# A routed-expert stage with 96 token columns per expert in place of 88

## The chip, the cores and the metric

The kernel runs on one core of one Trainium2 chip. The metric is device time in microseconds of one execution, the median of the runs. The profile is of one more execution of the same program, taken by the hardware profiler. Everything is float32.

## The reference, cut to what matters

A two-layer network is applied to 128 prompt tokens and 128 latent tokens. The second layer ends in a mixture of experts, and the change lies there:

```
logits = (xt @ w_router)                       # 8 experts
top_v, top_i = lax.top_k(logits, TOP_K)        # TOP_K = 2
top_w = jax.nn.softmax(top_v, axis=-1)
gate = sum(one_hot(top_i, N_EXPERTS) * top_w[..., None], axis=1)
for e in range(N_EXPERTS):
    out = out + gate[:, e:e+1] * swiglu(xt, wg[e], wu[e], wd[e])
# swiglu(x, wg, wu, wd) = (silu(x @ wg) * (x @ wu)) @ wd
```

The model width is 1024 and the hidden width of an expert is 2816. Each token goes to two of the eight experts, so 256 tokens make 512 pairs of token and expert, 64 per expert on average.

## The kernel before, in words

The two token groups run side by side (`NST = 2`, 256 tokens). Weights come through a ring of 11 tiles in SBUF (`ring`, `RING = 11`) of 1 MB each. The sync engine (SP) issues each tile's transfer when the slot's last reader has counted up `tile_used` and `tile_used0` (lines 433 to 441), and TensorE waits for the landing in `arrived` (line 607).

The expert stage works in units. A unit is one expert with room for `CAP` tokens: `SEL` is a 0/1 matrix that picks the tokens, `gather` (line 1362) multiplies by it to put up to `CAP` token columns into `XG`, and all that follows for the unit is `CAP` columns wide. Were an expert to have more than `CAP` tokens, the table built on VectorE (`OVER`, line 2629) would add further units for the same expert, which fetch the expert's weights once more. The loops run over units 0 to 6 and then from 7 to the number in the table, at least 8 and at most 13.

In a unit the hidden width is cut into steps of 1024, 1024, 512 and 256. Each step has a gate product and an up product (`across`, line 1394) and a down product (line 1415). All of them hold a 128x64 piece of a weight tile as the stationary operand and stream the token columns. They come in twos, one for each half of the 128 output rows (`HALVES`), so that the two halves of the array work at the same time. A float32 product is two records in the trace, so one pass of `for hp in HALVES` is two pairs of records. A tile is 64 records, a unit is 33 tiles or 2112 records, and eight units are 16896 records or 8448 pairs.

Between the products stand `turn_y` (line 1370, transposes of the unit's output before), `scatter` (line 1376, the output spread back over the tokens, twice two products of 512 columns), two transposes of `SEL` (line 1437), and the next unit's `gather`. ScalarE takes the gate products out of PSUM through SiLU (line 1878) and copies `YT`, `YG`, `SELT` and `XG`. VectorE multiplies by the up products (line 2664), adds the scattered output to `O` (line 2671), and makes the next `SEL` (line 2682). The order on each engine is the order of the code. The first seven units are unrolled on TensorE, so its program there is one long straight stream.

The block offsets in PSUM are multiples of `CAP`: four blocks side by side in a bank of 512 columns.

Of the kernel before, what the change touches and what calls it, by code (L numbers as in the profile page):

```python
# [38 lines left out]
NE = 8  # L39


CAP = 88
UNITS = NE + 5
STEPS = (1024, 1024, 512, TW)
UT = 33
# [129 lines left out]
def program(nc, t, out):  # L175
    ctx = ExitStack()
    with ctx:
        def sb(name, shape, dt=F32):
            return ctx.enter_context(nc.sbuf_tensor(name, shape, dt))
# [184 lines left out]
        TBL = sb("tbl", [P, 16], I32)  # L364
        SILU = W[5][:, 0:KC * CAP].rearrange("p (b n) -> p b n", b=2)
        HIDU = W[0][:, 0:2 * KC * CAP].rearrange("p (b c n) -> p b c n", b=2, c=KC)
        XG = W[1][:, 0:KC * CAP].rearrange("p (c n) -> p c n", c=KC)
        YG = W[1][:, 1024:2048]
        YT = W[4][:, 0:KC * CAP].rearrange("p (c n) -> p c n", c=KC)
        HTM = W[2][:, :].rearrange("p (s n) -> p s n", s=NST)  # L370
# [8 lines left out]
        IOTA = ROUTE[:, 384:512]  # L379
        SEL = ROUTE[:, 512:512 + NST * CAP].rearrange("p (s n) -> p s n", s=NST)  # L380
        SELT = ROUTE[0:CAP, 768:1024].rearrange("p (s n) -> p s n", s=NST)

# [2342 lines left out]
```

How the kernel before makes its waits and increments, by code:

```python
        @block.sync  # L427
# [3 lines left out]
            def tile(parts, i=None, per=0, dues=0):  # L431
                n = walk.n
                s, _ = walk.next(len(parts))
                if i is not None:
                    sp.wait_ge(sem("tile_used"), i * per + (n - RING + 1))
                    sp.wait_ge(sem("tile_used0"), i * per + (n - RING + 1))
                elif n >= RING:
                    sp.wait_ge(sem("tile_used"), tile_freed(tile_before(n)))
                for dst, src in parts:
                    sp.dma_start(dst(ring[:, s, :]), src).then_inc(sem(f"slot{s}"), 16)
# [49 lines left out]
            tile([whole(0, 1024, t["rw_w2"][0].rearrange("d k n -> (d k) n"))])  # L491
            tile([cols(t["rw_w_r"][0], TW)])
            tile([whole(0, 1024, t["rw_a2"][0], 64)])
            for n in range(2, 4):
                tile([cols(t["rw_w_r"][0], n * TW)])
            for n in range(4):
                tile([cols(t["rw_w_v"][0], n * TW)])
            tile([whole(0, 1024, t["rw_g2"][0])])
            for n in range(4):
                tile([cols(t["rw_w_o"][0], n * TW)])
            sp.wait_ge(sem("y"), 2 * KC)
            sp.wait_ge(sem("trk_done"), KC)
            ada_group(11)
            tile([(lambda s: s[:, 0:KC * NE].rearrange("p (k n) -> p k n", k=KC), kp(t["moe_router"][0]))])
# [31 lines left out]
                expert_tiles(u, u)  # L536
            walk.n = n0
            sp.wait_ge(sem("table"), 1)
            with sp.Fori(NE - 1, sp.value_load(TBL[0:1, UNITS:UNITS + 1], min_val=NE, max_val=UNITS)) as u:
```

## Time and profile before

| | us |
|---|---|
| median of 3 runs | 1753.9 |
| lowest and highest | 1748.24 and 1754.79 |
| the profiled execution's own time | 1753.9 |
| its span, first to last instruction | 1752.1 |
| TensorE busy | 1604.5 (92%) |
| VectorE, ScalarE, GpSimd busy | 530.2, 297.4, 16.4 |
| products of lines 1394 and 1415, busy | 448.9 and 224.6 |
| granted TensorE clock, mean | 0.970 |

The expert stage is the last 790 us of the span. The page's line of slices shows it as the stretch where the DMA digit is 9 from slice 22 on, where TensorE is also at 9, and where VectorE and ScalarE are at 0 and 1. Two numbers that look alike are not: the mean time of a product (240 ns) is how long one is under way, and the products overlap, so their pace is read from how many start in a stretch.

### The profile page before, as it was taken

The page shows a single profiled execution, that of the slowest core. Times are in us where ns is not written, and L with a number is a line of the kernel's source. Part 1 is how long each engine was busy: PE and PEld are TensorE (multiplying, and loading weights), DVE is VectorE, ACT ScalarE, POOL GpSimd, SP SyncE. Part 2 cuts the span into 40 slices and gives each one's busy share as a digit, 9 for nine tenths or more (in the row PEclk, how much of TensorE's full clock was granted, in tenths as well). Part 3 has the DMA queues.
Part 4 walks back from the last instruction along what each step waited for, and adds up shares of the span by engine and source line. Part 5 has one row for each costly group of instructions (what it writes and reads, how often), then busy time and mean ns, then how long its engine had stood idle before and what let it go on. Part 6 is the DMA issues. An engine that isn't in the chain of part 4 may idle for free.

```text
span 1752.1 us, 59234 instructions
## 1 busy us (share of the span) xinstructions
PE 1604.5 (92%) x27345; PEld 1420.5 (81%) x27345; DVE 530.2 (30%) x1253; ACT 297.4 (17%) x684; POOL 16.4 (1%) x32
## 2 busy tenths in 40 slices
PE   3999898999979999999687999999999999999996
PEld 1888477999447888898577989898989899898885
DVE  0363425667453436656524100000010101000001
ACT  1111413101023413343204001010100000010001
POOL 1000000000000000000000000000000000000000
PEclk9999998999999999999886999999999999999998
DMA  9832697545584420000433999999999999999990
GB/s 333 257 97 76 205 305 240 187 151 192 170 255 117 132 73 5 5 7 7 140 108 142 340 382 347 365 347 366 359 363 362 367 366 374 366 360 371 333 338 25
DMA packets 212032, 408.94 MB, mean 233 GB/s; under 512 B 13090, under 2 KB 135252, under 8 KB 211796
## 3 DMA queue, kind: packets, MB, share of 16 engines
q1 hardware_dynamic: 207344, 398.91, 64.1%
q8 instruction: 215, 3.52, 0.8%
q0 software_dynamic: 1184, 3.41, 0.7%
q10 hardware_dynamic: 3268, 2.93, 0.5%
q14 instruction: 21, 0.17, 0.0%
HBM read 403.30 MB, written 1.92 MB: 231 GB/s over the span
## 4 chain that ended last, share of the span: by engine, by line
PE 47%; PEld 40%; issue 5%; DVE 4%; ACT 2%; SPq 1%; DMA 1%; DVEq 0%; POOL 0%; PEldq 0%; ACTq 0%
PEld bank L1394 25%; PEld bank L1415 12%; PE bank L945 8%; PE bank L976 4%; PE bank L631 3%; PE bank L628 3%; PE bank L722 3%; PE bank L725 2%; PE bank L1155 2%; PE bank L1115 2%; PE bank L656 2%; PE bank L747 2%; PE bank L1151 2%; PE bank L1140 2%; PE bank L1091 2%
## 5 line engine op out<-in xcount | busy, mean ns | idle before, releaser
L1394 PEld LDWEIGHTS bank<-w,ring 128*64 128x64 f32 x11264 | 435.7, 137 | 43.0 <-issue 42.2
L1394 PE MATMUL bank<-w,ring 128*64 128x88 f32 x11264 | 448.9, 240 | 22.5 <-issue 21.5
L1415 PE MATMUL bank<-w,ring 128*64 128x88 f32 x5632 | 224.6, 240 | 11.7 <-issue 11.5
L1415 PEld LDWEIGHTS bank<-w,ring 128*64 128x64 f32 x5632 | 217.0, 137 | 17.9 <-issue 17.2
L2664 DVE TENSOR_TENSOR w<-w,bank 128x352 f32<-128x352 f32 (+1 forms) x48 | 22.1, 488 | 615.1 <-PE bank L1394 615.1
L1878 ACT ACTIVATE w<-bank 128x352 f32<-128x352 f32 (+1 forms) x48 | 19.3, 437 | 461.6 <-PE bank L1394 461.5
L628 PE MATMUL bank<-w,ring 128*128 128x256 f32 x256 | 57.6, 387 | 5.8 <-DVE w L2342 5.2
L656 PE MATMUL bank<-ring,ct 128*32 128x256 f32 x768 | 48.2, 405 | 15.7 <-DMA ring<-in_ada_w 14.0
L628 PEld LDWEIGHTS bank<-w,ring 128*128 128x128 f32 x256 | 49.4, 194 | 14.0 <-DVE w L2342 5.5
L631 PE MATMUL bank<-ring,w 128*128 128x256 f32 x256 | 58.1, 391 | 0.9 <-DVE w L1942 0.9
L631 PEld LDWEIGHTS bank<-ring,w 128*128 128x128 f32 x256 | 50.2, 197 | 8.5 <-DVE w L1942 1.3
L656 PEld LDWEIGHTS bank<-ring,ct 128*32 128x32 f32 x768 | 25.4, 116 | 35.3 <-issue 20.0
L1155 PE MATMUL bank<-ht 64*64 64x64 f32 x1280 | 49.7, 219 | 0.0
L2671 DVE SCALAR_TENSOR_TENSOR o<-bank,w,o 128x512 f32<-128x512 f32 x32 | 24.0, 751 | 84.3 <-PE bank L1376 82.2
L722 PE MATMUL bank<-ht,ring 128*128 128x256 f32 x192 | 45.3, 394 | 2.2 <-ACT ht L1532 2.2
L722 PEld LDWEIGHTS bank<-ht,ring 128*128 128x128 f32 x192 | 37.0, 196 | 8.3 <-ACT ht L1532 2.4
L1155 PEld LDWEIGHTS bank<-ht 64*64 64x64 f32 x1280 | 43.3, 135 | 0.5
L945 PE MATMUL bank<-ht,ring 128*128 128x128 f32 x352 | 43.0, 275 | 0.7 <-ACT gb L1539 0.7
L945 PE MATMUL bank<-w 128*128 128x128 f32 x352 | 42.9, 275 | 0.0
L945 PE MATMUL bank<-w,ring 128*128 128x128 f32 x352 | 42.9, 275 | 0.0
L725 PE MATMUL bank<-ring,ht 128*128 128x256 f32 (+1 forms) x192 | 41.9, 371 | 0.0
L945 PEld LDWEIGHTS bank<-ht,ring 128*128 128x128 f32 x352 | 41.1, 192 | 0.9 <-ACT gb L1539 0.9
(420 smaller groups left out, 1984.3 us busy)
## 6 DMA issues: line engine op xcount, KB each, us to landing
ring<-in_moe_w_gate SPq DMA_DIRECT2D x88, 1024.0 KB, 6.7
ring<-in_moe_w_up SPq DMA_DIRECT2D x88, 1024.0 KB, 7.1
ring<-in_moe_w_down SPq DMA_DIRECT2D x88, 1024.0 KB, 7.0
ring<-in_ada_w SPq DMA_DIRECT2D x48, 1024.0 KB, 6.2
ring<-in_ev_w_in SPq DMA_DIRECT2D x11, 1024.0 KB, 12.0
ring<-in_ffn_w_gate SPq DMA_DIRECT2D x11, 1024.0 KB, 7.8
ring<-in_ffn_w_up SPq DMA_DIRECT2D x11, 1024.0 KB, 5.3
ring<-in_ffn_w_down SPq DMA_DIRECT2D x11, 1024.0 KB, 6.5
```

What stands on the lines that cost most here:

```text
L628: ins = mm(b[:, a * TW:(a + 1) * TW], w[:, k, a * P:(a + 1) * P], src[:, k, :], start=k == 0, stop=k == KC - 1)
L631: ins = mm(b[:, a * TW:a * TW + n], src[:, k, a * P:(a + 1) * P], w[:, k, 0:n], start=k == 0, stop=k == KC - 1)
L656: ins = mm(sums_bank(n)[32 * j:32 * j + 32, 0:TW], CT[:, NST * k:NST * k + 32], w[:, k, :], start=k == 0, stop=k == KC - 1)
L722: ins = mm(b[:, a * TW:(a + 1) * TW], w[:, k, a * P:(a + 1) * P], HT[:, k, :], start=k == 0, stop=k == KC - 1)
L725: ins = mm(b[:, a * TW:a * TW + n], HT[:, k, a * P:(a + 1) * P], w[:, k, 0:n], start=k == 0, stop=k == KC - 1)
L747: ins = mm(bank[2 + 2 * (n % 2) + h][:, j * P:(j + 1) * P], KG[hp, seg], WQ[hp, seg] if lv else W[0][hp, qs], start=True, stop=True)
L945: ins = mm(region(j, r)[:, which * P:(which + 1) * P], lhs(which, k), rhs(k), start=first and which == 0 and k == 0, stop=k == 3, skip_gro ...
L976: ins = mm(bank[DOWN_BANK[p]][:, :], lhs, rhs, start=n == 0, stop=n == FT - 1)
L1091: ins = mm(bank[7 - n % 2][:, a * TW:(a + 1) * TW], XS["v"][:, k, a * P:(a + 1) * P], held["w"][:, k, :], start=k == 0, stop=k == KC - 1)
L1155: ins = mm(bank[2 + d][hp, (4 + j) * DH:(5 + j) * DH], IZ[hp, d, j, :], IP[i % 2][hp, d, j, :], start=True, stop=True)
L1394: ins = [mm(b[hp, (a % 4) * CAP:(a % 4 + 1) * CAP], w[:, k, a * P + hp.start:a * P + hp.stop], XG[:, kk, :], start=kk == 0 and a % 4 == 0, ...
L1415: ins = [mm(bank[4 + c // 4][hp, (c % 4) * CAP:(c % 4 + 1) * CAP], w[:, k, c * P + hp.start:c * P + hp.stop], HIDU[:, s % 2, 2 * part + k, :],
```

## The change

One constant is raised by eight. Every width that is written with `CAP` follows it: the streamed columns at lines 1362, 1394 and 1415, the width of the copies and multiplications at lines 1858, 1863, 1878, 1891, 2597, 2664 and 2682, the rows at 1370, 1376, 1437, 1883, 1886 and 1903, and the thresholds at lines 2629 and 2633. No instruction is added, removed or moved on any engine; all 803 rows of TensorE's order stand where they stood, with other sizes, and SP's order is the same word for word. Four blocks of 96 columns still fit in a bank of 512.

```
-CAP = 88
+CAP = 96
 UNITS = NE + 5
 STEPS = (1024, 1024, 512, TW)
```

## Rows read from the trace of the kernel before

**Rows 1.** The page: chain that ended last, by engine.
```profile
PE 47%; PEld 40%; issue 5%; DVE 4%; ACT 2%; SPq 1%; DMA 1%; DVEq 0%; POOL 0%; PEldq 0%; ACTq 0%
```

**Rows 2.** Windows: the expert stage, and 95 us of it; columns in the first line.
```profile
core 0: us, PE busy (x) PEld busy (x) DVE busy (x) ACT busy (x) POOL busy (x), PEclk, DMA share, GB/s
960.80:1731.10 770.30, 735.65 (x17296) 697.23 (x17296) 57.06 (x137) 62.02 (x118) 0.00 (x0) 1.00 0.94 347
1067.00:1162.00 95.00, 90.48 (x2130) 85.47 (x2128) 6.55 (x14) 8.07 (x15) 0.00 (x0) 1.00 0.97 359
```

**Rows 3.** The page: transfers by tensor, size, issue to landing.
```profile
ring<-in_moe_w_gate SPq DMA_DIRECT2D x88, 1024.0 KB, 6.7
```

**Rows 4.** Waits of SP's queue, 975 to 1731 us: total, times, longest.
```profile
SPq L437 <- PE bank L1394: 368.1, 168, 4.0
SPq L437 <- PE bank L1415: 193.5, 81, 7.0
```

**Rows 5.** TensorE's waits, 972.3 to 1731.1 us: total, times, longest.
```profile
PE bank L1394 <- issue: 21.5, 34, 1.8
PE bank L1415 <- issue: 11.5, 21, 1.2
PE bank L1362 <- issue: 0.9, 1, 0.9
```

**Rows 6.** Timeline, 1098 to 1135 us: start, us, what, idle before.
```profile
1103.58 1.12 PE L1415 MATMUL bank<-w,ring 128*64 128x88 f32 x23
...
1105.32 5.07 PE L1415 MATMUL bank<-w,ring 128*64 128x88 f32 x128 [0.62 <-issue]
1105.32 4.91 PEld L1415 LDWEIGHTS bank<-w,ring 128*64 128x64 f32 x128 [0.79 <-issue]
...
1117.02 5.07 PE L1394 MATMUL bank<-w,ring 128*64 128x88 f32 x127 [1.23 <-issue]
...
1128.25 5.07 PE L1415 MATMUL bank<-w,ring 128*64 128x88 f32 x128 [0.68 <-issue]
```

**Rows 7.** DMA queues, 975 to 1725 us: packets, MB, share.
```profile
q1 hardware_dynamic: 88451, 262.03, 93.9%
q8 instruction: 133, 2.18, 1.1%
```

**Rows 8.** DMA queues, 800 to 850 us.
```profile
q8 instruction: 11, 0.18, 1.6%
q10 hardware_dynamic: 540, 0.12, 1.3%
```

**Rows 9.** Timelines at three widths: 64, 88 and 512 columns.
```profile
807.32 0.63 PE L1151 MATMUL bank<-ht 64*64 64x64 f32 x16
807.79 0.63 PE L1155 MATMUL bank<-ht 64*64 64x64 f32 x16
...
985.73 9.93 PE L1394 MATMUL bank<-w,ring 128*64 128x88 f32 x256
995.59 1.98 PE L1376 MATMUL bank<-w 88*128 88x512 f32 x4
...
434.67 1.88 PE L976 MATMUL bank<-w 128*128 128x512 f32 x4
436.39 1.02 PE L976 MATMUL bank<-ring,w 128*128 128x512 f32 x2
```

**Rows 10.** Timelines: full weight loads with 128 and with 88 columns.
```profile
324.90 1.95 PE L945 MATMUL bank<-w 128*128 128x128 f32 x16
326.68 1.95 PE L945 MATMUL bank<-w,ring 128*128 128x128 f32 x16
...
1143.62 3.81 PE L1362 MATMUL bank<-w 128*128 128x88 f32 x32
```

**Rows 11.** Instructions by form, 972.3 to 1731.1 us: ScalarE, then VectorE.
```profile
L1878 ACT ACTIVATE w<-bank 128x352 f32<-128x352 f32 x40 | 16.8, 461 | 305.9 <-PE bank L1394 305.8
L1878 ACT ACTIVATE w<-bank 128x176 f32<-128x176 f32 x8 | 2.5, 317 | 155.7 <-PE bank L1394 155.7
...
L2664 DVE TENSOR_TENSOR w<-w,bank 128x352 f32<-128x352 f32 x40 | 19.4, 518 | 486.8 <-PE bank L1394 486.8
```

**Rows 12.** The last of the pauses, 1697 to 1706 us.
```profile
1702.48 3.02 PE L1394 MATMUL bank<-w,ring 128*64 128x88 f32 x73 [1.77 <-issue]
```

## The prediction

> **What bounds the kernel now.** I read the chain of waits first: 87% of it is TensorE and its weight loads [rows 1]. Then I cut out the stage that the change touches. The expert stage, from the first product of line 1394 to the last of line 1415, is 770.3 us of the span of 1752.1, TensorE is busy for 735.65 of them, and the transfers are at a share of 0.94 [rows 2]. Both look like a bound, and the whole case hangs on which it is.
>
> If transfers were the bound, wider products would hide behind them. They are not, and two views say so. SP spends 368.1 + 193.5 = 561.6 us of this stage waiting for TensorE to give back a slot, never more than 7.0 us at a time [rows 4]. So a tile is asked for when the one 11 places before it is done. It lands 6.7 us later in the median [rows 3]. A tile is 64 products, 2.43 us at the pace found below, so its turn comes more than 20 us after it was asked for, and it lies ready for some 15 to 20 us. The transfers run at TensorE's speed because TensorE gives out the slots. They are nearly full all the same, which matters below.
>
> How many units run? The gate weights are fetched 88 times, 11 tiles for each of 8 units [rows 3]. Eight is the least the table can give. No expert has more than 88 tokens, and the larger room saves nothing.
>
> **TensorE's pace by width.** Lines 1394 and 1415 put two products on the two halves of the array, and I count in pairs. At 88 columns 256 records start in (9.93 - 0.24) us, 128 pairs, 75.7 ns each (75.8 by the starts inside a run) [rows 9]. At 64 columns 16 records start every 0.47 us, 58.4 ns a pair. At 512 columns, one product at a time, four start in 1.72 us, 430 ns each [rows 9]. From 88 to 512 that is (430 - 75.8)/424 = 0.835 ns per column, two passes at 2.4 GHz, and 75.8 is 88 x 0.833 + 2.5. So what is streamed sets the pace at 88. The load of a 64-column weight is no bound there, since the same load fits in 58.4 ns at 64 columns. Hence 96 columns take 96 x 0.833 + 2.5 = 82.5 ns, 6.67 ns more per pair.
>
> Term 1: 8448 pairs x 6.67 ns = +56.3 us. Its bounds: the slope from 64 to 88 columns, 0.73 ns, gives 5.8 ns and +49; if the fixed part grew from 2.5 to the 5 ns seen at 64 columns, the pair takes 85.0 ns and the term is +78. I take +56.
>
> The Trainium skill has another figure for a stream of weight loads and products (TensorE: Matmul & The Clock Gate, "Back-to-back issue gap"): about 81 ns at 128 columns and 131 ns at 512, because the loads are pipelined with the products. By it a column costs 0.13 ns, 16 more streamed columns per pair (two passes) cost 2.1 ns, and the term would be 8448 x 2.1 = +18 us. The rows at 88 and 512 columns speak against it.
>
> **The pauses, which give some of it back.** TensorE is idle in the stage for 21.5 + 11.5 + 0.9 = 33.9 us in 56 pieces, all marked issue [rows 5]. It isn't the ring (tiles lie ready), and no engine releases it. The timeline shows what they are: 128 products with their 128 weight loads, a pause, 128 more, a pause [rows 6]. 256 instructions also are what one packet of the instruction queue brings: 133 packets move 2.18 MB, 16.4 KB each, 64 bytes an instruction [rows 7]. All but two of these pauses stand at the same place in a block of 256 instructions when the stream is counted from its start. The next block of TensorE's program is late. A product's record stays open for 0.24 us, so the true loss is some 0.17 us more per pause. Read off the starts it is 46 us, in 64 pauses of over 0.2 us from 979.9 to 1702.5 us, the longest 1.8 [rows 6, 12].
>
> A block of 128 products runs 64 x 75.8 = 4.85 us. Pauses of 0.6 us, the common ones, mean that a block took 5.4 to 5.5 us to come, and the long ones 6 to 6.6. In the scan at 800 to 850 us the same products' worth of instructions (128 at 29.2 ns, 3.7 us a block) came at 3.7 us without a pause, with the data queues at 1.3% [rows 8, 9]. So the fetch is slowed by the weight traffic that it shares the engines with.
>
> With 96 columns a block runs 64 x 82.5 = 5.28 us, 0.43 us longer. Each pause shrinks by that or goes. Done pause by pause over the 64, 51 stay, with 21 us in them. That is the upper value if the fetch is as slow as now. But TensorE then asks for a tile every 2.64 us of a run and not every 2.43, 397 GB/s and not 431, so the queue in front of the fetch is shorter. If that takes another 0.4 us from the fetch, 8 us remain; another 0.2, 13 us. The ends are 46 (nothing shrinks) and 0. I take 14.
>
> Term 2: 46 - 14 = 32 us given back.
>
> The Trainium skill (Runtime: NRT & Kernel Launch, "Instruction fetch mechanics") says that instructions come in blocks of 256 and that crossing a block boundary is mostly hidden. The block size is that of the rows; hidden it isn't here. If the pauses had another cause, as that would suggest, nothing would be given back, which is the second rival below.
>
> **The small edits.** The gather (32 products in 3.81 us) runs at 112 to 119 ns a product with 88 columns, the same as 111.7 ns for 128 columns with the same full load [rows 10], so its 8 more columns are free: bounds 0 and 9 gathers x 32 x 6.67 ns = 1.9 us, taken 0. The scatter streams 512 columns whatever `CAP` is. ScalarE's copies grow by (461 - 317)/176 = 0.8 ns a column, 26 ns for 32 more [rows 11]; VectorE's by about as much. Both engines are busy for 62 and 57 us of 770 and wait for TensorE [rows 2, 11]. The few copies that TensorE waits for, two at the start and four at the end of the stage, add 0.1 us. Selecting tokens before the stage has two instructions of 8 more columns, under 0.02 us. Loads are the same in number and size. Nothing before the stage changes.
>
> **The sum.** +56.3 - 32 + 0.2 (with the first 4 us of the stage at half clock) = +24.5 us. The profiled execution took 1753.9 us, as did the median, so 1778.5 us; the span would be 1776.6.
>
> **The rivals.**
> 1. *The fetch gets out of the way altogether.* Slower traffic shortens it below 5.28 us in every block. For it: most pauses are under 0.7 us, within reach of 0.43 plus a little. Against it: 16 of the 64 pauses are over 1 us, and that is not a small excess. The pauses go to 3 us or less: 56.3 - 44 = +12, 1766 us.
> 2. *The pauses stay.* Their cause isn't the fetch, or it slows with the stream: +56, 1810 us. The same place in every block speaks against it.
> 3. *The pair has a larger fixed part* (85.0 ns). A block runs 5.44 us, more of the pauses go (10 us remain): 78 - 36 = +42, 1796 us. For it: 64 and, with full loads, 128 columns show 5 ns over the stream; but there a weight load of the same length explains it.
> 4. *Faster.* The place is the seam between weight load and stream: if loads and not columns set the pair, as the flatter slope would have it, a pair grows by 2.1 ns (+18), and if the thinner traffic still ends all the pauses (-46), the kernel takes 1726 us. It decides at 46 us / 8448 = 5.4 ns a pair: below that and with all pauses gone it is faster. The slope of 0.835 ns speaks against the first half, and with 2.1 ns a block only 0.13 us longer the second half hardly follows.
> 5. *Nothing happens* since the transfers are the bound: 0, 1754 us. SP's waits speak against it.
>
> **How the numbers follow.** Forecast (pauses left between 5 and 25 us) 0.68; rival 1 0.12; rival 2 0.05; rival 3 0.07; rival 4 0.02; rival 5 0.06. The forecast's own range is 56.3 - 41 to 56.3 - 21, +15 to +35, 1769 to 1789. The range has to take in most of rival 1: 1764 to 1791. A measurement can tell about 0.5% from no change, 8.8 us. Slower by more than that: 0.68 + 0.12 + 0.05 + 0.07 = 0.92. Within: rival 5, 0.06. Faster: 0.02.
>
> **What would show it.** In the profile after: 256 records of line 1394 in a run take 10.8 us, not 9.93 (128 x 82.5 ns + 0.24; 11.1 would be rival 3, 10.2 rival 4). The gate weights are still fetched 88 times. SP still waits for TensorE for over 500 us. Between pauses there still are 128 products, and the waits marked issue for lines 1394 and 1415 sum to 5 to 15 us, in 20 to 50 pieces. The stage takes about 795 us. The gather stays at 3.8 us. I am wrong in the bound if tiles are waited for, wrong in term 1 if the run of 256 isn't near 10.8 us, and wrong in term 2 if the pauses stay above 25 us.

## The result and the profile after

The changed kernel takes 1768.65 us (median of 10 runs, 1763.4 to 1769.69), the kernel before 1754.35 us beside it (10 runs, 1748.24 to 1763.58). The ratio is 1.0065, 95% interval 1.0041 to 1.009: slower by some 11 us, 14 us between the medians. The forecast was +24.5 us. The direction and the range held; the size was off by about a factor of two (24.5 against 14.3 or 11). The profiled execution took 1767.48 us with a span of 1765.7, 13.6 us over that of before, and the account below is made in those two executions.

The stage in one window of the profile after (columns as in [rows 2]):

```profile
core 0: us, PE busy (x) PEld busy (x) DVE busy (x) ACT busy (x) POOL busy (x), PEclk, DMA share, GB/s
960.10:1744.60 784.50, 778.38 (x17296) 747.57 (x17296) 59.04 (x142) 64.08 (x118) 0.00 (x0) 1.00 0.92 341
```

It grew from 770.1 to 784.4 us, first start to last start of a product. Over it the transfers average 341 and not 347 GB/s. The pace, from the timeline after:

```profile
984.46 10.78 PE L1394 MATMUL bank<-w,ring 128*64 128x96 f32 x256
995.17 1.98 PE L1376 MATMUL bank<-w 96*128 96x512 f32 x4
...
1047.24 3.81 PE L1362 MATMUL bank<-w 128*128 128x96 f32 x32
```

256 products take 10.78 us where they took 9.93 [rows 9]; (10.78 - 0.25)/128 is 82.3 ns, and 82.5 ns by the starts inside a run. The gather takes the same 3.81 us with eight more columns [rows 10]. TensorE's waits in the stage (total, times, longest) and the page's row of gate weights:

```profile
PE bank L1394 <- issue: 3.2, 5, 0.8
PE bank L1415 <- issue: 2.8, 4, 1.4
```

```profile
ring<-in_moe_w_gate SPq DMA_DIRECT2D x88, 1024.0 KB, 6.3
```

The 56 waits and 33.9 us of [rows 5] have become 9 waits and 6.0 us. The unit count is the same (88 tiles), and tiles land a little sooner, 6.3 us after they are asked for and not 6.7. Two of the pauses that are left, still with a block's end in front of them (113 and 15 products, 128, lie between the two):

```profile
1036.07 4.86 PE L1415 MATMUL bank<-w,ring 128*64 128x96 f32 x113 [0.65 <-issue]
1040.75 0.82 PE L1394 MATMUL bank<-w,ring 128*64 128x96 f32 x15
1042.39 4.92 PE L1394 MATMUL bank<-w,ring 128*64 128x96 f32 x113 [0.82 <-issue]
```

Counted over all of TensorE's instructions in the trace, 62 of the 63 pauses over 0.25 us before and 11 of the 12 after stand at one place (instruction 193 or 194) of a block of 256. And 62 and 11 end 2.2 to 2.7 us after the start of a packet of 16,384 bytes on the instruction queue q8, 256 instructions of 64 bytes. So all but one of the pauses in each trace end with the arrival of a block.

The account, all from distances between starts of products in the two traces:

| | before | after | difference |
|---|---|---|---|
| products at their pace (75.8 and 82.5 ns a pair) | 638.8 | 695.3 | +56.5 |
| pauses over 0.25 us (63 and 12) | 44.3 | 8.2 | -36.1 |
| distances of 0.1 to 0.25 us, their excess | 5.4 | 3.2 | -2.1 |
| rest within the products | 2.4 | -0.8 | -3.2 |
| gather, scatter, transposes | 79.3 | 78.5 | -0.8 |
| stage | 770.1 | 784.4 | +14.3 |
| before the stage | | | -0.7 |

Part of the rest is luck of one execution. Before, the first 3.5 us of the stage ran at the granted clock of 1.2 GHz (the row's 0.51), after at 2.4 GHz (1.00), 48 against 86 products:

```profile
960.80:964.30 3.50, 3.45 (x48) 3.46 (x50) 2.95 (x17) 2.10 (x3) 0.00 (x0) 0.51 0.02 5
```

```profile
960.20:963.70 3.50, 3.50 (x86) 3.50 (x88) 2.95 (x17) 2.04 (x3) 0.00 (x0) 1.00 0.02 5
```

### The profile page after: what moved, and what is told of

Same layout as the page of the kernel before. It is cut to its first block, busy times and chain, and to the rows that moved or that the text cites. A ratio compares the mean times of both kernels' runs of the same rounds, so it can differ in the third digit from the quotient of the medians.

```text
span 1765.7 us, 59234 instructions
## 1 busy us (share of the span) xinstructions
PE 1646.2 (93%) x27345; PEld 1469.7 (83%) x27345; DVE 530.8 (30%) x1253; ACT 299.8 (17%) x684; POOL 16.4 (1%) x32
## 4 chain that ended last, share of the span: by engine, by line
PE 46%; PEld 42%; DVE 4%; issue 3%; ACT 2%; SPq 1%; DMA 1%; DVEq 0%; PEldq 0%; POOL 0%; ACTq 0%
PEld bank L1394 26%; PEld bank L1415 13%; PE bank L945 8%; PE bank L976 4%; PE bank L631 3%; PE bank L628 3%; PE bank L722 3%; PE bank L725 2%; PE bank L1155 2%; PE bank L1115 2%; PE bank L656 2%; PE bank L747 2%; PE bank L1151 2%; PE bank L1140 2%; PE bank L1091 2%
## 5 line engine op out<-in xcount | busy, mean ns | idle before, releaser
L1394 PEld LDWEIGHTS bank<-w,ring 128*64 128x64 f32 x11264 | 468.0, 137 | 19.4 <-issue 18.4
L1394 PE MATMUL bank<-w,ring 128*64 128x96 f32 x11264 | 476.7, 246 | 3.9 <-issue 3.2
L1415 PE MATMUL bank<-w,ring 128*64 128x96 f32 x5632 | 239.0, 246 | 2.8 <-issue 2.8
L1415 PEld LDWEIGHTS bank<-w,ring 128*64 128x64 f32 x5632 | 234.2, 137 | 5.9 <-issue 4.9
L2664 DVE TENSOR_TENSOR w<-w,bank 128x384 f32<-128x384 f32 (+1 forms) x48 | 23.6, 518 | 620.9 <-PE bank L1394 620.9
L1878 ACT ACTIVATE w<-bank 128x384 f32<-128x384 f32 (+1 forms) x48 | 20.5, 462 | 460.4 <-PE bank L1394 460.3
```

Of the source, the lines that this page charges most:

```text
L1394: ins = [mm(b[hp, (a % 4) * CAP:(a % 4 + 1) * CAP], w[:, k, a * P + hp.start:a * P + hp.stop], XG[:, kk, :], start=kk == 0 and a % 4 == 0, ...
L1415: ins = [mm(bank[4 + c // 4][hp, (c % 4) * CAP:(c % 4 + 1) * CAP], w[:, k, c * P + hp.start:c * P + hp.stop], HIDU[:, s % 2, 2 * part + k, :],
```

## The experiments

The theory after the result: the columns cost all that was forecast (6.67 ns a pair), and the pauses gave more of it back than forecast. They are fetches of TensorE's instruction blocks, slowed by the weight traffic. Rivals: something else than the streamed columns moved; the pauses depend on the block's length alone; they depend on the traffic's queue. The kernel before ran beside each set of experiments, 19 to 29 times, with medians of 1757.9 to 1760.37 us; the ratios are the numbers to compare. Each kernel has one trace. The three traces of kernels whose products stream 88 columns under the full traffic (before, the first and the control experiment) show 44.3, 50.5 and 51.6 us of pauses over 0.25 us and stages of 770.1, 774.3 and 778.5 us, so a single stage time is good to some 8 us there.

**The columns alone undone.** The changed kernel, with 88 of the 96 columns streamed.

```
-ins = [mm(b[hp, (a % 4) * CAP:(a % 4 + 1) * CAP], ..., XG[:, kk, :], ...
+ins = [mm(b[hp, (a % 4) * CAP:(a % 4) * CAP + 88], ..., XG[:, kk, 0:88], ...
 ... (and the same at line 1415)
```

> The changed kernel, but the products of lines 1394 and 1415 stream 88 of the 96 columns (columns 88 to 95 of each block are not computed); gather, copies, multiplications, layout and thresholds stay at 96. Theory (the streamed columns are the whole cost, and the wider copies are hidden): the run of 256 products is back at 9.93 us, the waits marked issue of lines 1394 and 1415 are back at 30 to 36 us in 50 to 60 pieces, and the time is that of the kernel before, 1750 to 1758 us, ratio 0.998 to 1.003. Rival (some of the added time comes from the wider copies, the layout at a pitch of 96 or the gather): 1760 us or more, ratio at least 1.004.

Measured: 1756.55 us, ratio 0.9989 (0.9964 to 1.0014). A pair is back at 75.8 ns and the issue waits at 39.7 us in 52 pieces, more than the 30 to 36 expected. The wider copies, the pitch of 96 and the gather cost nothing that can be told (the interval is some 4 us wide to either side).

**A quarter of the traffic, at both widths.**

```
-etile((lambda slot: slot.rearrange("p (k n) -> p k n", n=n), src))
+m = n * 1 // 4
+etile((lambda slot: slot.rearrange("p (k n) -> p k n", n=n)[:, :, 0:m], src[:, :, 0:m]))
 ... (and the same in the down tiles)
```

> The kernel before, with a quarter of each expert weight tile fetched (the rest of the slot keeps what it held, so the expert outputs are not the reference's); instructions and semaphores are the same in number and order. Theory (the pauses are fetches of blocks of 256 instructions of TensorE that are slowed by the weight traffic): the waits marked issue in the expert stage fall from 33.9 to under 3 us, the pair stays at 75.8 ns, the stage takes 720 to 726 us and the execution 1704 to 1711 us, ratio 0.972 to 0.976. Rival (the pauses belong to the instruction stream itself, whatever the traffic): they stay at 30 us or more and the time at 1750 to 1758 us. Second rival (they go in part, since tiles arrive in bunches): 1715 to 1745 us.

> The changed kernel with a quarter of each expert weight tile fetched (the same part left out as in the run before it). Theory: without pauses the whole price of the columns is seen, 8448 pairs x 6.67 ns = 56 us over the same kernel with 88 columns: stage 776 to 781 us, execution 1757 to 1764 us, ratio to the kernel before 1.002 to 1.006. Rival (the columns cost only the 14 us that the change showed, and the pauses are not what hid the rest): 1718 to 1730 us where the 88-column kernel takes about 1708, or no gain from the missing traffic in both.

Measured at 88 columns: 1705.23 us, ratio 0.9697 (0.9668 to 0.9725), stage 720.2 us. At 96: 1755.74 us, ratio 0.9983 (0.9969 to 0.9997), stage 775.0 us. These kernels leave out three quarters of each expert tile. The queues from 975 to 1670 us and TensorE's only wait from 972.3 to 1678 us, at 88 columns:

```profile
q1 hardware_dynamic: 88190, 65.27, 32.5%
q8 instruction: 131, 2.15, 1.3%
```

```profile
PE bank L1397 <- issue: 0.4, 1, 0.4
```

Line 1397 is line 1394 of before. The instruction packets still come, one for each block, and of the pauses of [rows 5] a single one of 0.4 us is left. The data packets come in full number too (88190; 88451 in the somewhat longer stretch of [rows 7]), each smaller, so it is their bytes or the time they take, and not their count, that delays the fetch. Without pauses eight columns cost 50.5 us of time and 54.8 us of stage, nearly all of the 56 expected. The first time lay within what was expected, the second 1.3 us under it (1757 to 1764). Both ratios lay under their ranges, for these had been worked out from a kernel before of 1754 us, and it took 1760 beside them.

**One step on, 104 columns.**

```
-CAP = 96
+CAP = 104
```

> The same edit taken one step on, 104 columns. Theory (pairs at 2 x 104/2.4 + 2.5 = 89.2 ns, and the pauses, 8 us at 96 columns, have nothing more to give): the stage takes 784 + 56 - 8 to 784 + 56 us, the execution 1814 to 1824 us, ratio to the kernel before 1.034 to 1.040, waits marked issue under 3 us, 256 products in 11.6 us. Rival (each 8 columns cost what the change cost, 14 us): 1779 to 1785 us.

Measured: 1813.5 us, ratio 1.03 (1.0268 to 1.0331). The run, and the one wait marked issue that is left:

```profile
985.61 11.63 PE L1394 MATMUL bank<-w,ring 128*64 128x104 f32 x256
```

```profile
PE bank L1394 <- issue: 0.2, 1, 0.2
```

The ratio lies under the range expected, for it was worked out from a kernel before of 1754 us, and the runs of it beside this kernel took 1760; the time lies 0.5 us under its own. Against the changed kernel's profile the stage grew by 47.3 us (831.7), a little under the 48 to 56 expected. The next eight columns cost three times what the first did.

**Thinner traffic at the old width.** 59 of every 64 columns of each tile are fetched, so that runs of products ask for the bytes per us that they ask for with 96 columns.

```
+m = n * 59 // 64
```

> The kernel before with 59 of every 64 columns of each expert weight tile fetched (the last 5 of 64 keep what the slot held, so the expert outputs are not the reference's). Width 88 and a block of 4.85 us as before, but in a run of products the transfers are asked for at 397 GB/s in place of 431, as with 96 columns. This parts the two ways in which 96 columns can shorten the pauses. Theory (both work, the thinner traffic by about 0.3 us a fetch): pauses longer than 0.25 us fall from 44 us (the page's issue waits from 33.9) to 20 to 32 us, the time falls by 12 to 24 us against the kernel before, ratio 0.986 to 0.993. Rival (only the longer block counts): 44 us of pauses stay, ratio 0.998 to 1.002. Second rival (only the traffic counts): 8 us stay, ratio 0.977 to 0.982.

Measured: 1728.57 us, ratio 0.9833 (0.9777 to 0.9889), pauses over 0.25 us 20.6 us in 33 pieces. The waits (lines 1394 and 1415 of before):

```profile
PE bank L1397 <- issue: 7.4, 13, 1.5
PE bank L1418 <- issue: 6.4, 9, 1.2
```

The pauses are where the theory put them. The time is a little lower than it said, between it and the second rival, and its interval reaches into the rival's range. 8% less traffic halves the pauses while the blocks run as short as before.

The delay itself can be read from the starts in the traces, 975 to 1670 us: from the first instruction of a block to the start of the next instruction packet (median). A pause follows where this and some 2.4 us more, from the packet's start to the end of the pause, are longer than the block.

| kernel | us to the packet's start |
|---|---|
| 88 columns (three traces) | 2.9, 3.1, 3.0 |
| 88 columns, a quarter of the traffic | 0.6 |
| 88 columns, 59 of 64 | 2.3 |
| 96 columns | 2.1 |
| 104 columns | 1.8 |

**Fewer tiles under way.** First the control, with SP's loop written out, then the same with a wait on the landing of the tile two places before.

```
-with sp.Fori(0, NE - 1) as u:
+for u in range(NE - 1):
+    walk.n = n0
     expert_tiles(u, u)
 ...
```

```
 sp.wait_ge(sem("tile_used0"), i * per + (n - RING + 1))
+if isinstance(i, int):
+    b, due = issued[-2]
+    sp.wait_ge(sem(f"slot{b}"), due)
 ...
```

> The kernel before with SP's loop over the first seven units written out, nothing else: the control for the run after it. All theories: as before within 0.3%, pauses of 40 to 50 us, for SP isn't the bound. If SP's registers and branches did delay transfers, the weights would come in thicker bunches and the pauses would grow by a few us.

> The written-out kernel with one more wait on SP: a tile of the first seven units is asked for only once the tile two places before it has landed, so that at most two are under way. The amount of traffic is the same, only the queue in front of an instruction fetch is shorter. Theory (the fetch waits behind queued weight packets, and 96 columns shortened that queue): landing falls from 6.7 to 4.5 to 5.5 us, pauses from 44 to under 20 us, time 1722 to 1740 us where the kernel before takes 1754, ratio 0.981 to 0.992. Rival (the fetch is slowed by the rate of the traffic, not by its queue): pauses stay within 5 us of the control and so does the time. Third way (two under way can't feed TensorE): it waits for tiles, the time is above the control's.

Measured: control 1756.6 us, ratio 0.9986 (0.9962 to 1.001); with the wait 1761.35 us, 1.0014 (0.9987 to 1.0042). SP now waits for landings and hardly for TensorE (33 us in all), and a tile lands 5.7 to 5.9 us after it is asked for, where the control has 6.9 to 7.4 and 4.5 to 5.5 was expected:

```profile
SPq L440 <- DMA ring<-in_moe_w_down: 184.1, 73, 4.6
SPq L440 <- DMA ring<-in_moe_w_up: 182.6, 71, 4.5
SPq L440 <- DMA ring<-in_moe_w_gate: 175.5, 68, 4.6
```

```profile
PE bank L1399 <- issue: 21.6, 30, 1.5
PE bank L1420 <- issue: 17.5, 21, 1.2
```

The issue waits are 39.1 us in 51 pieces (39.8 in the control; pauses over 0.25 us 50.5 against 51.6). My theory fell here: the queue of tiles was shortened and nothing came of it. It was shortened less than it sounds, since the control has only 2.5 tiles under way on average (at most 4) and the kernel with the wait 2.0 (over the seven units that it governs). But that is fewer than with 96 columns (2.1) or with thinner tiles (2.2), which have 8.2 and 20.6 us of pauses against 50.5, and the delay to the instruction packet is 2.9 us against the control's 3.0. So how many tiles are ahead is not what shortens the pauses. The share of the transfers stayed at 0.96, as the rival has it; that it is the rate and nothing else of the traffic isn't shown.

**Narrower: 80, 64 and 92 columns.** In the first two the threshold for further units is out of reach, so that eight units run; at 64 columns the tokens of an expert beyond 64 are left out.

```
-CAP = 96
+CAP = 80
 ...
-v.tensor_scalar(OVER[:, cut], TAKEN, float((level + 1) * CAP), None, ALU.is_gt)...
+v.tensor_scalar(OVER[:, cut], TAKEN, 1.0e6, None, ALU.is_gt)...
```

> The edit made the other way, 80 columns, with the number of units held at 8 (the threshold for further units is out of reach, so tokens beyond 80 of an expert are left out). Theory: the pair takes 69.2 ns, 56 us less in all; a block would run 4.43 us, but the next comes after 5.4 us, so nearly every block of a run has a pause: pauses of 85 to 110 us in over 90 pieces, time 1742 to 1765 us, ratio 0.993 to 1.006. Rival (pauses stay at 44 us as they have another cause): 1698 us, ratio 0.968. Between them (only the 64 blocks with pauses lose 0.43 us more): 1725 us, ratio 0.984.

> 64 columns, with the number of units held at 8 (tokens beyond 64 of an expert are left out). The products need 58.3 ns a pair, 148 us less than at 88. Theory (the traffic of the weights sets a floor, and TensorE feels it through its instruction blocks, which come no faster than every 5.4 us while the transfers are at 0.97): the rate stays at 355 to 375 GB/s, pauses of 190 to 250 us, time 1735 to 1765 us, ratio 0.986 to 1.004, and tiles still lie ready when their turn comes. Rival (TensorE now waits for tiles, the plain bound by transfers): the same time, but the waits name DMA of ring and not issue. Second rival (the fetch gets faster as TensorE does less): below 1700 us.

> The edit made half-way, 92 columns. Theory (88 columns still stand on the floor that the traffic sets, the price of a column comes in gradually): the products take 28 us more, pauses over 0.25 us fall from 44 to 18 to 26 us, time 0 to 8 us above the kernel before, ratio 1.000 to 1.005. Rival (every column costs its 7 us): ratio 1.014 or more.

Measured, with the kernels of above in their places (products: 8448 pairs at the pace of the trace; pauses over 0.25 us and stage from the traces):

| columns | products at their pace | pauses | stage | ratio to before (95%) |
|---|---|---|---|---|
| 64 | 492 | 166.2 | 775.3 | 1.0007 (0.9988 to 1.0026) |
| 80 | 585 | 96.7 | 773.1 | 1.0028 (0.9998 to 1.0057) |
| 88 | 640 | 44.3 | 770.1 | 1 |
| 92 | 669 | 25.8 | 777.8 | 1.0008 (0.9986 to 1.0029) |
| 96 | 697 | 8.2 | 784.4 | 1.0065 (1.0041 to 1.009) |
| 104 | 754 | 0.4 | 831.7 | 1.03 (1.0268 to 1.0331) |

Gathers and the like add 78 to 81 us to each. All three widths came out as the theory had it in time; at 64 the pauses are shorter than the 190 to 250 us expected, though 100 of the 102 again end 2.2 to 2.7 us after the start of an instruction packet. The same stretch, 975 to 1670 us, at 64, 80, 88 (before), 92 and 96 (after) columns, columns as in [rows 2]:

```profile
975.00:1670.00 695.00, 550.62 (x15234) 513.51 (x15235) 42.31 (x100) 48.55 (x103) 0.00 (x0) 0.96 0.98 357
```

```profile
975.00:1670.00 695.00, 617.27 (x15439) 578.67 (x15437) 46.88 (x102) 52.18 (x103) 0.00 (x0) 0.99 0.98 359
```

```profile
975.00:1670.00 695.00, 663.02 (x15600) 627.11 (x15598) 48.31 (x102) 54.62 (x105) 0.00 (x0) 1.00 0.97 362
```

```profile
975.00:1670.00 695.00, 677.25 (x15459) 644.99 (x15456) 48.83 (x102) 54.86 (x103) 0.00 (x0) 1.00 0.97 358
```

```profile
975.00:1670.00 695.00, 688.90 (x15321) 661.64 (x15316) 46.67 (x98) 55.77 (x103) 0.00 (x0) 1.00 0.96 355
```

TensorE has 127 us less to do at 64 than at 92 columns, and starts no more products. The rate is 357 to 362 GB/s from 64 to 92 columns. Eleven of the 264 tiles land before the stage. The other 253, 265.3 MB, take 753, 747, 742 and 748 us at 64, 80, 88 and 92 columns from the first request to the last landing, 3 to 5 us after the stage's start to 19 to 25 us before its end: that is the flat part of the table. And yet TensorE never waits for a tile there. At 64 columns:

```profile
PE bank L1394 <- issue: 101.8, 66, 3.1
PE bank L1415 <- issue: 48.7, 34, 3.0
```

```profile
SPq L437 <- PE bank L1394: 374.2, 165, 5.3
SPq L437 <- PE bank L1415: 193.9, 81, 6.1
```

SP still waits for TensorE to give back slots, and each tile lies landed for at least 15 us. Part of the row at 64 columns is the clock: the granted clock fell to 1.2 GHz in 17 short stretches, 61 us in all (hence the 0.96); just before the first of them TensorE had paused for 2.0 us. It cost some 27 us of the stage (an estimate: products that take 31 us at 58.4 ns a pair took 58 us there). That is a small part of the 148 us that the narrower products save, and the rest went into pauses.

**More traffic at the new width.** A further 88 KB beside each tile, into a part of SBUF that nothing reads.

```
+b, a = ...
+sp.dma_start(W[b][:, a:a + 176], t["moe_w_gate"][0][0][0:P, 0:176]).then_inc(sem(f"slot{s}"), 16)
-w = arrived(i=u, per=48)
+w = arrived(2, i=u, per=96)
 ...
```

> The changed kernel with one more transfer of 88 KB beside each expert tile, into a part of SBUF that nothing reads, and TensorE waits for both: a width of 96 with 8.6% more traffic, in a run of products 431 GB/s asked for as at 88. It is the other corner to the kernel with 88 columns and thinner traffic. Theory (longer block and thinner traffic each did a part): pauses over 0.25 us go from 8 back to 15 to 30 us, time 7 to 22 us above the changed kernel, that is 1775 to 1790 us where the kernel before takes 1757, ratio 1.010 to 1.020. Rival (the longer block did all): pauses stay at 8 us, ratio 1.005 to 1.008. Second rival (the traffic did all): 35 us of pauses or more, ratio over 1.022.

Measured: 1796.85 us, ratio 1.0206 (1.0177 to 1.0235), stage 814.3 us, pauses over 0.25 us 35.9 us in 45 pieces. That is more than the theory said, at the edge of the second rival:

```profile
q1 hardware_dynamic: 114008, 263.03, 98.7%
```

```profile
PE bank L1397 <- issue: 19.1, 27, 1.7
PE bank L1418 <- issue: 8.9, 16, 1.1
```

I had the size of the extra traffic right and not its effect. The stage's 288 MB took 784 us from the first request to the last landing, at a share of 98.7% and in a third more packets than the 85499 of the kernel before. So it may sit on a floor of its own, some 40 us higher, and it isn't the clean corner that I wanted. It shows that traffic brings the pauses back (the delay to the instruction packet is 3.1 us again, where 96 columns have 2.1); by how much at equal load it doesn't.

## Why the prediction was wrong

**Right: the columns.** 82.5 ns a pair was forecast and measured, 256 products in 10.8 us forecast and 10.78 measured, +56.3 and +56.5 us. Eight units, a free gather and hidden copies held too; the first experiment undid the columns alone and had the old time back. The Trainium skill's flatter figure (TensorE: Matmul & The Clock Gate, "Back-to-back issue gap"), by which a column costs 0.13 ns, is not what this kernel shows: from 80 to 104 columns a column costs a pair 0.83 ns, 0.42 for each of its two passes.

**The step that failed: term 2, "I take 14".** 46 us of pauses were to become 14, and 8 are left (44.3 to 8.2 by the count over 0.25 us). The cause was the right one, and the quarter-traffic kernels show it. The first half of the step, a block that runs 0.43 us longer, was sized from the trace. The second, the relief from thinner traffic, had no row. By my own steps (0.2 us leaves 13 us, none leaves 21) the 14 us stand for a little under 0.2 us a fetch. Thinning alone, at 88 columns, brought 44.3 us down to 20.6. Taking 0.4 us from every pause of the kernel before leaves as much, and with the pauses of the other two traces at 88 columns it takes 0.55 to 0.6 us, so the relief was two to three times what I took. The delay to the instruction packet, read directly, fell by more: from 2.9 to 3.1 us down to 2.3 with the thinner tiles and 2.1 with 96 columns. With 0.43 and 0.4 us together the sum over the pauses of before leaves 7 us: 8.2 are seen. The end of my own range for the relief, 0.4 us, had 8 us next to it. The waits marked issue were forecast at 5 to 15 us in 20 to 50 pieces and came to 6.0 us in 9, and the stage at about 795 us took 784.4.

**What the sum left out.** Some 7 us beside the pauses, with the 0.7 before the stage: the small distances (-2.1), the rest (-3.2, of which about 1.7 is the clock at the start, different in the two executions), gather and the like (-0.8). Together with the 4 us of the pauses that is the difference between 24.5 and 13.6. So only part of the miss is the failed step, and the rest lies in terms taken as nothing. Rival 1 (1766 us, 0.12) came nearest, though the pauses did not quite go.

**Half right: what bounds the kernel.** I wrote that the transfers are no bound, since SP waits for TensorE and tiles lie ready. Both are so, and at 64 columns they are still so, while the time doesn't fall by anything that can be told for 148 us less of products. From 64 to 92 columns the stage stays at 770 to 778 us and the transfers at 357 to 362 GB/s. As I read it, the traffic reaches TensorE not through the ring but through its instructions: a block of instructions comes late, TensorE gives back slots later, and the weights go no faster. The packets' times and the kernels with less traffic show the first link; that the loop settles at this rate, and why, is argued. Rival 5 had "nothing happens since the transfers are the bound" and was argued away by SP's waits; they can't tell the two apart. It would have been the right answer for 92 columns. At 96 TensorE's own 697 + 79 us and what is left of the pauses come out above the floor of 770 to 778. From 96 to 104 columns the products cost 57 us more and the last 8 us of pauses went, and beyond that no pause is left to pay for a column.

The Trainium skill (DMA: Bandwidth & Descriptors, "Specifications") gives about 358 GB/s as what a core can draw from HBM. The rows at 357 to 359 GB/s are close to it; the kernel before passes it over the same 695 us (362), and the kernel with extra traffic reaches 371. The Trainium skill's "mostly hidden" for the crossing of an instruction block (Runtime: NRT & Kernel Launch, "Instruction fetch mechanics") holds here at a quarter of the traffic and does not in the kernel before, where the transfers' share over the stage is 0.94.

**Open.** The instruction packets themselves take 1.0 us in the kernel before and 1.1 us with a quarter of the traffic, and from their start to the end of a pause it is 2.2 to 2.7 us throughout, so what grows with the traffic (0.6 to 3 us) lies ahead of the packet's start. What holds it up there, and which property of the traffic does, wasn't tried. No version that fetches all of the weights beat the kernel before; 64, 80, 88 and 92 columns are the same to the measurement, and of those 88 and 92 hold the most tokens.

## What to carry to other kernels

Slots that lie full and a transfer queue that waits for TensorE do not prove that the transfers are free: look at the rate as well, and at waits marked issue that come every 256 instructions, for the weights may be starving the instruction stream. Where both needs are close (here a stage that stays at 770 to 778 us with the transfers near 360 GB/s, against 719 us of products, gathers and the like), size an edit by the larger of the two and not by either alone. Work that was added to the smaller was free here up to 92 columns (747 us of TensorE's own), and at 96, where the two needs meet at some 776 us, 8 us of pauses came on top. And a feedback that the trace shows (longer blocks, thinner traffic, quicker fetch) deserves one worked number of its own before it is given a round one.

## What the runs showed of the hardware

- A pair of float32 products on the two column halves starts every 2 N / 2.4 + 2.5 ns at N = 80, 88, 92, 96 and 104 (69.2, 75.8, 79.2, 82.5 and 89.2 ns within a run) at the granted clock of 2.4 GHz, and its 64-column weight loads are hidden.
- With a product of a full 128-column load the pace is 112 ns (median) at 64, 80, 88, 96, 104 and 128 columns alike.
- An instruction block for TensorE, 128 products with their loads, came within 4.85 us at 97 GB/s of weight traffic, and at some 360 GB/s about half of them took longer, 5.4 to 6.6 us (4.85 us and the pause). Its packet of 16,384 bytes started 0.6 us (median) after the block before it began in the first case and 2.9 to 3.1 us in the second, and TensorE went on 2.2 to 2.7 us after that start in both. Cutting the tiles under way from 2.5 to 2.0 on average, at the same rate, changed nothing.
- At 64 columns, with pauses of up to 3.1 us, the granted clock fell to 1.2 GHz for 61 us of the stage, at 92 columns and above in none of it from 975 us on.
- 8% less traffic alone, with the same work on TensorE, was worth 1.7% of the time (ratio 0.9833).
